# Feed-forward products by half products, with the convolution's sums in PSUM

## What is computed

```python
def conv_ffn(h, w_up, conv_w, conv_b, w_down, rows):
    u = h @ w_up                                   # (512, 1024) @ (1024, 5632)
    u = conv2d_grid(u, conv_w, rows) + conv_b      # 3x3, each channel by itself
    gate, val = jnp.split(u, 2, axis=-1)           # 2816 channels each
    return (jax.nn.silu(gate) * val) @ w_down      # (512, 2816) @ (2816, 1024)
...
        h = modulate(rms_norm(x, norm2_g[l]), sh2, sc2)
        x = x + g2 * conv_ffn(h, ffn_w_up[l], ffn_conv_w[l], ffn_conv_b[l], ffn_w_down[l], rows)
```

## Time and profile before

| | us |
|---|---|
| runs of the kernel before | 2051.56, 2053.72, 2055.73 |
| median | 2053.72 |
| the profiled execution's own time | 2056.36 |
| its span | 2054.4 |
| feed-forward, first to last up product | 582.95 to 889.10 |
| feed-forward, down products | 889.10 to 1065.20 |

### The profile page before, as it was taken

One profiled execution on the slowest core, in us unless ns is written; L12 is line 12 of the kernel. 1 busy time (PEld: TensorE's weight loads), 2 busy tenths in 40 slices (PEclk: granted clock), 3 DMA queues, 4 the chain that ended last, 5 costly groups with the idle time before them and its releaser, 6 DMA issues. The chain is left out here.

```text
span 2054.4 us, 27368 instructions
## 1 busy us (share of the span) xinstructions
PE 1844.3 (90%) x11650; PEld 1047.3 (51%) x11650; DVE 938.7 (46%) x1560; ACT 401.8 (20%) x740; POOL 152.0 (7%) x223
## 2 busy tenths in 40 slices
PE   6999759788999999999979999989988988878887
PEld 3554338676434444444538888865565333233332
DVE  2564196354349888950028559954443110101013
ACT  3222443234120111010113111253022000000001
POOL 0000002850000000000001100010000000000000
PEclk8999979798999999999989999999998999999999
DMA  8344004322311221135225522230538999999996
GB/s 318 139 184 153 21 21 108 82 53 78 106 60 67 82 82 68 63 102 193 87 82 200 210 103 82 98 109 21 208 149 319 427 426 426 426 426 425 427 427 251
DMA packets 80909, 375.40 MB, mean 183 GB/s; under 512 B 34336, under 2 KB 37408, under 8 KB 56848
## 3 DMA queue, kind: packets, MB, share of 16 engines
q1 hardware_dynamic: 68480, 344.56, 43.1%
q0 software_dynamic: 9552, 27.73, 3.8%
q10 hardware_dynamic: 2752, 1.31, 0.2%
HBM read 360.65 MB, written 18.87 MB: 185 GB/s over the span
## 5 line engine op out<-in xcount | busy, mean ns | idle before, releaser
L3113 PE MATMUL psum<-mem 128*64 128x512 f32 x1504 | 356.5, 630 | 36.3 <-DMA mem<-in_w_upe 16.3
L1962 PE MATMUL psum<-mem 128*128 128x512 f32 x704 | 305.0, 595 | 2.0 <-ACT mem L377 2.0
L1752 PE MATMUL psum<-mem 128*128 128x256 f32 x1120 | 250.4, 383 | 9.3 <-ACT mem L2330 4.9
L3113 PEld LDWEIGHTS psum<-mem 128*64 128x64 f32 x1504 | 117.9, 144 | 254.4 <-issue 250.9
L2028 DVE SCALAR_TENSOR_TENSOR mem<-mem 128x512 f32<-128x512 f32 x352 | 237.1, 750 | 0.0
L1752 PEld LDWEIGHTS psum<-mem 128*128 128x128 f32 x1120 | 212.7, 191 | 47.5 <-issue 13.9
L1962 PEld LDWEIGHTS psum<-mem 128*128 128x128 f32 x704 | 133.7, 190 | 172.7 <-issue 171.3
L574 PE MATMUL psum<-mem 128*128 128x512 f32 (+1 forms) x464 | 167.6, 523 | 2.1 <-ACT mem L377 2.0
L1408 PE MATMUL psum<-mem 128*128 128x512 f32 x352 | 156.0, 600 | 1.2 <-ACT mem L1984 1.2
L574 PEld LDWEIGHTS psum<-mem 128*128 128x128 f32 x464 | 87.9, 190 | 81.1 <-issue 72.1
L3175 DVE TENSOR_TENSOR mem<-mem,psum 128x512 f32<-128x512 f32 x16 | 11.0, 688 | 248.5 <-issue 217.9
(11 more groups left out here) (383 smaller groups left out, 2125.0 us busy)
## 6 DMA issues: line engine op xcount, KB each, us to landing
mem<-in_w_upe SPq DMA_DIRECT2D x31, 2048.0 KB, 27.5
mem<-in_w_gate SPq DMA_DIRECT2D x30, 2048.0 KB, 29.1
mem<-in_w_downe SPq DMA_DIRECT2D x29, 2048.0 KB, 32.2
mem<-in_ada SPq DMA_DIRECT2D x32, 1024.0 KB, 6.8
mem<-in_w_up SPq DMA_DIRECT2D x22, 1024.0 KB, 4.8
mem<-in_ada POOLq DMA_DIRECT2D x32, 512.0 KB, 4.8
mem<-in_w_in_g SPq DMA_DIRECT2D x12, 1024.0 KB, 4.9
mem<-in_w_down SPq DMA_DIRECT2D x16, 704.0 KB, 4.1
```

Source lines behind the costliest of these rows:

```text
L1752: last = pe.matmul(self.bank(q, n), left[:, kt], right[:, kt], start=n in (1, 2, 5) and kt == 0, stop=kt == self.tiles - 1, skip_group_che ...
L1962: last = pe.matmul(k.bank[2 * (m % 3) + h2][:, :], w[:, kt, h2], h[:, kt], start=kt == 0, stop=kt == KD - 1)
L3113: last = pe.matmul(bank[halves[h], :], xs[:, kt, halves[h]], pair[h][0][:, kt, cols], start=kt == 0, stop=kt == tiles - 1, skip_group_chec ...
```

## The change

The up products go by `Seven`, one pair for each m (gate tile and value tile, 4 input tiles in a quarter); the down products by `SevenDown`, four pairs of output tiles, 11 input tiles in a quarter. The weight quarters of the down products no longer pass through the ring: they have places of their own, which `SevenDown.load` fills (704 KB each). `x1` is updated in place.

The work around them moves:

- ACT reads out seven half results per pair (`take`): four into the padded grids, the three to be joined into `part`. It also starts each convolution: the centre tap with the bias, from the grid into a PSUM bank (`centre`).
- DVE does eight taps for each half, onto the sum in PSUM (banks 4 to 7); the last tap of the value half writes to SBUF. It makes t1 to t4 at the start.
- POOL makes the weight sums s1 to s4 of each pair, the three joins (`add`) and the product into `hidden`.
- The side jobs move to other places of the down half: all modulation rows stand between its first products.

```diff
+class SevenDown(SevenResidual):
...
+    def load(self, sp, q, i, j):
+        if (i, j) == (0, 0) and q:
+            sp.wait_ge(self.done[1], q)
+            sp.wait_ge(self.summed, 4 * q)
...
+        sp.dma_start(self.slot(q, i, j), self.source(q, i, j)).then_inc(self.landed[i, j], 16)
...
+    def sum_1(self, eng, q):
+        if q:
+            eng.wait_ge(self.done[7], q)
+            eng.wait_ge(self.summed, 4 * q)
...
+        eng.tensor_tensor(self.s1, self.block(q, 1, 0), self.block(q, 1, 1), ADD).then_inc(self.summed, 1)
...
+    def sum_3(self, eng, q):
+        eng.wait_ge(self.done[5], q + 1)
+        eng.tensor_tensor(self.s1, self.block(q, 0, 0), self.block(q, 1, 0), SUB).then_inc(self.summed, 1)
...
         @block.gpsimd
...
+            def add(q, n):
+
+                h2, j, other = {2: (0, 0, 1), 3: (0, 1, 6), 7: (1, 1, 5)}[n]
+                at = pads.half(h2, q, j)
+                pool.wait_ge(up.taken[other], q + 1)
+                pool.wait_ge(up.taken[n], q + 1)
+                pool.tensor_tensor(at, at, rows4(pads.part[n]), ADD).then_inc(s["added"], 1)
+
+            def product(m):
+                pool.wait_ge(s["silu"], m + 1)
+                pool.wait_ge(s["tap_v"], NT * (m + 1))
+                pool.tensor_tensor(hidden[:, m], pads.silu[m % 2], pads.value[m % 2], MUL).then_inc(s["hidden"], 1)
...
+            for q in range(KF):
+                if q:
+                    add(q - 1, 7)
+                if q >= 3:
+                    product(q - 3)
+                add(q, 2)
+                if q < LAST:
+                    landed(q + 1)
+                    up.sum_1(pool, q + 1)
+                    up.sum_2(pool, q + 1)
+                add(q, 3)
+                if q < LAST:
+                    up.sum_4(pool, q + 1)
+                    up.sum_3(pool, q + 1)
+                if q == LAST - 1:
+                    down.sum_1(pool, 0)
+            add(LAST, 7)
+            product(LAST - 2)
+            pool.wait_ge(up.done[4], KF)
+            pool.wait_ge(s["hidden"], 11)
+            down.turn_1(pool)
+            down.sum_2(pool, 0)
+            down.sum_4(pool, 0)
+            product(LAST - 1)
+            down.sum_3(pool, 0)
+            product(LAST)
 
         @block.tensor
...
+            for q in range(KF):
+                k.weights_ready(pe, k.number("w_up", q))
+                for n in (1, 2, 5, 6):
+                    up.product(pe, q, n, (lambda kt, first=4 * (n - 1): apply.ready(pe, first + kt, 0)) if q == 0 and n < 3 else None)
+                if q:
+                    up.product(pe, q - 1, 4)
+                up.product(pe, q, 3)
+                up.product(pe, q, 7)
+            up.product(pe, LAST, 4)
...
+            down.product(pe, 0, 1)
...
+            mod.rows_by_product(pe, range(4))
+            pe.wait_ge(up.taken[4], KF)
+            down.product(pe, 0, 5)
+            mod.rows_by_product(pe, range(4, 8))
+            pe.wait_ge(s["hidden"], KF)
+            down.product(pe, 0, 2)
+            mod.turn(pe)
...
         @block.scalar
...
+            def centre(h2, m):
+                act.wait_ge(s["added"], 3 * m + 2 + h2)
...
+                t = m + KF * h2
+                act.activation(pads.sums[h2](m), pads.inner(h2, m), ACT.Identity, bias=k.v("ffn_conv_b", t),
+                               scale=k.v("ffn_conv_w", CENTRE * 2 * KF + t)).then_inc(s[("centre_g", "centre_v")[h2]], 1)
...
+            for q in range(KF):
+                if q:
+                    centre(0, q - 1)
+                take(q, 1)
+                take(q, 2)
+                if q >= 2:
+                    silu(q - 2)
+                take(q, 5)
+                take(q, 6)
+                if q:
+                    take(q - 1, 4)
+                    centre(1, q - 1)
+                take(q, 3)
+                take(q, 7)
...
         @block.vector
...
+            def tap(h2, m, i):
+                done, centre = (s[("tap_g", "tap_v")[h2]], s[("centre_g", "centre_v")[h2]])
+                if i == 0:
+                    dve.wait_ge(centre, m + 1)
+                else:
+                    dve.wait_ge(done, NT * m + i)
...
+                dve.scalar_tensor_tensor(out=out, in0=pads.shifted(h2, m, TAPS[i]), scalar=w, in1=a, op0=MUL, op1=ADD).then_inc(done, 1)
...
+                if kt == 6:
+                    dve.wait_ge(apply.done, 4)
+                    up.turn_1(dve)
...
+            for m in range(KF + 1):
+                for i in range(NT):
+                    if m < KF:
+                        tap(0, m, i)
+                    if m:
+                        tap(1, m - 1, i)
```

More of the change, by code:

```diff
@@ L1942, in _, with landed @@
             sp.dma_start(context.x, k.d["ctx2"]).then_inc(context.landed, 16)
+            down.load(sp, 1, 0, 1)
             k.send_weights(sp)
+            for q in range(2, ND):
+                down.load(sp, q, 0, 1)
+                down.load(sp, q, 0, 0)
+                down.load(sp, q, 1, 0)
+                down.load(sp, q, 1, 1)
         @block.gpsimd
         def _(pool):
-            pool.memset(k.at(work, NP * 2 * PADW), 0.0).then_inc(s["zeroed"], 1)
-            pool.memset(mod.c32, 0.0).then_inc(s["zeroed"], 1)
+            def landed(q):
+                g = k.number("w_up", q)
+                pool.wait_ge(k.w_loaded[g % RING], 16 * (g // RING + 1))
@@ new lines, in _ @@
+            down.product(pe, 0, 3)
+            down.product(pe, 0, 7)
+            for q in range(1, ND):
+                down.product(pe, q, 1)
+                down.product(pe, q, 2)
+                if q == 2:
+                    context.sum(pe, 2)
+                down.product(pe, q, 5)
+                if q == 3:
+                    context.spread(pe)
+                down.product(pe, q, 6)
+                if q < 3:
+                    context.sum(pe, (0, 3)[q - 1])
+                down.product(pe, q - 1, 4)
+                down.product(pe, q, 3)
+                norm.sum(pe, 2 * q - 2)
+                down.product(pe, q, 7)
+                if q == 1:
+                    context.sum(pe, 1)
+                norm.sum(pe, 2 * q - 1)
@@ L1966, in _ @@
+            down.product(pe, ND - 1, 4)
+            norm.sum(pe, KD - 2)
             norm.sum(pe, KD - 1)
@@ new lines, in _, with square @@
+            centre(0, LAST)
+            take(LAST, 4)
+            centre(1, LAST)
+            silu(LAST - 1)
+            mod.take_rows(act, 0)
+            mod.take_rows(act, 1)
+            silu(LAST)
+            mod.take_rows(act, 2)
+            mod.take_rows(act, 3)
+            warm_root(k, act)
+            def square(m):
+                down.tile_done(act, m)
+                norm.square(act, m, x1[:, m])
+            act.wait_ge(mod.turned, 1)
+            square(0)
+            context.square(act, 0)
@@ L2000, in _ @@
+            context.square(act, 1)
+            square(1)
+            square(2)
+            context.square(act, 2)
+            context.square(act, 3)
+            context.take_root(act)
+            for m in range(3, KD):
+                square(m)
             act.wait_ge(s["total"], 1)
@@ new lines, in _ @@
+            add(0, 1)
+            dve.wait_ge(s["hidden"], KF)
+            down.turn_2(dve)
+            add(0, 5)
+            down.turn_3(dve)
+            add(0, 2)
+            add(0, 6)
+            down.turn_4(dve)
+            add(0, 3)
+            add(0, 7)
+            for q in range(1, ND):
+                down.sum_1(dve, q)
+                down.sum_2(dve, q)
+                down.sum_4(dve, q)
+                if q == 1:
+                    mod.add(dve)
+                add(q, 1)
+                add(q, 2)
+                add(q, 5)
+                down.sum_3(dve, q)
+                add(q, 6)
+                if q == ND - 1:
```

328 lines of the change are left out of this document (173 added, 155 removed).

## The result

| | before | changed |
|---|---|---|
| median of 4 runs each, one chip, us | 2054.56 (2051.56 to 2055.73) | 1997.72 (1991.55 to 2002.72) |
| ratio to before, 95% interval | | 0.9724 (0.9693 to 0.9755) |
| profiled execution, its span | 2056.36, 2054.4 | 1999.77, 1997.9 |
| feed-forward, from its first product to the start of the final norm's last product, its spread (L1970, now L2130) | 488.99 | 434.73 |
| of it up | 306.15 | 269.63 |

The change takes 56.8 us off the median. In the two profiled executions the feed-forward stage lost 54.3 us of the 56.6 between them. The rest is not the change's: the stage starts 2.7 us earlier (580.22 against 582.95), behind the same work, and what follows it is 0.5 us longer.

What follows compares the result with a forecast made beforehand. PE was taken to bound both feed-forward halves. Savings of 36.0 us up and 19.3 down sum to 55.3 off the 2053.7 us median, giving 1998.4, stated as 1999 us; range 1989 to 2025.

Steps and rivals of the forecast that it cites:

- A pair at 12.12 us: Up half: seven half products, 56 instructions at 0.2164 us, take 12.12 us of PE per pair.
- Up half: From first up product to the down half: 270.1 us instead of 306.15, so 36.0 us saved.
- The start: Start of the up half: 3.0 us lost, bounds 1.6 and 6, as product 2 waits for the eighth applied tile.
- The tap's period: Up half on DVE: sixteen taps a pair at 0.674 us, 10.8 us in all; high end 0.79 each, 12.6 us.
- rival (a): Up half: DVE becomes the bound at 0.79 us a tap, 11 us more, 2010 us in all; chance 0.12.
- GpSimd and ACT: Up half, per pair: GpSimd 8.2 us, about 8.9 with hand-overs, and ACT 5.1, both under 12.12.
- Rival (b): Up half: ACT or GpSimd holds PE 1 us each pair, 22 us more, 2021 us in all; chance 0.11.
- Contention: DVE taps beside GpSimd: no time charged, since taps have one operand in PSUM; only turns and weight sums at the start collide.
- Rival (c): Up half: taps and GpSimd exclude each other for whole instructions, 19.7 us a pair, 2165 us in all; chance 0.05.
- Down half: Down half: products 133.3 us instead of 151.4, saving 18.1; net saving with waits and tail 19.3 us.
- the wait for the rows' weights: Between the halves: PE waits 1.5 us, bounds 0 and 5, for the last weight tiles of the modulation rows.
- Rival (d): More gain: the 4.6 us at a lower clock and the start's 3 do not arise, 1992 us; chance 0.05.

Runs made afterwards that it cites:

- the eighth half product: Changed kernel with an eighth half product, its result unused, added to each up pair: 2027.19 us in one run.
- the two extra additions: Changed kernel with two more 512-word additions on GpSimd in each up pair: 1994.0 us; with four more, 2031.56 us.
- the rows moved alone: Changed kernel with the last two groups of modulation rows moved behind down product 2, GpSimd's order unchanged: 1999.64 us in one run.
- both moves: Changed kernel with half the modulation rows behind down product 2 and GpSimd's last product into `hidden` ahead of sum s3: median 1993.26 us, ratio 0.9723.

## Why the prediction was right

*The total.* 1997.7 us against 1999 forecast is closer than the sum behind it: the stage saved 54.3 us and not 55.3, the up half half a microsecond more and the down half 1.6 less, while the profiled executions differ by 56.6, of which 2.3 lie outside the stage. So the last microsecond or two of the match is luck; the mechanism is judged by the stage.

*A pair at 12.12 us.* Right to the digit, and the eighth half product shows that it is PE's time. Up half 269.6 us against 270.1 forecast: saved 36.5 against 36.0.

*The start.* 269.63 - 22 x 12.12 - 0.5 = 2.5 us lost, 3.0 forecast. It is the wait for the eighth tile, as forecast: ACT ends that tile at 585.39, where the forecast's time from the first product gives 585.5. PE's clock is 0.50 (1.2 GHz) until 584, as it was at the start of the stage before, but the tile comes later still. The turns did collide with GpSimd there, t1 too, which the prediction had left out (the sum beside it took 2.17 us). It cost PE nothing, though narrowly: t2 ends at 587.52, and the first weight load of product 6 is at 587.64.

*DVE.* The tap's period is 0.659, at the low end of the range; it decides rival (a) against. The reason given for it, that no tap needs the one right before it, is borne out too: the last pair's value taps have no gate taps between them, and seven of them take 864.82 - 859.29 = 5.53 us, 0.79 each, the figure of rival (a).

*GpSimd and ACT.* GpSimd's 512 words were mis-sized, 1.28 us against 1.17, and its 256 words 0.69 against 0.79; together 8.5 us a pair, within the 8.2 to 8.9 given. ACT's 7 x 0.384 + 2 x 0.78 + 0.59 = 4.8 against 5.1. Rival (b) is excluded by the waits and by the two extra additions. It is real at 13.6 us.

*Contention.* Nothing charged, and nothing found in steady state. Rival (c) was real for another placement of the sums, and priced 2.7 us a pair too dear (19.7 against 17.0), since it charged whole durations.

*Down half.* Saved 17.7 us against 19.3, and its terms were off in both directions. More time than forecast: the wait for the rows' weights 3.1 instead of 1.5; products at a lower clock 139.1 - 133.3 = 5.8 instead of the 4.6 kept from before (the row's 139.4 holds two instructions of the last up product); `mod.turn` in the same low stretch 4.8 instead of 3.9. Less: the last down product 4 did not wait (0.5; idle before L1723 is 0.1), the norm's sums and its spread are 1.0 shorter in busy time (5.1 and 1.6 us for 5.6 and 2.1), and the context's sums and spread 0.3. In sum -19.3 + 1.6 + 1.2 + 0.9 - 0.5 - 1.0 - 0.3 = -17.4, within 0.3 of what was measured. The wait of 1.2 before the first down product is gone as well, but it lay in the up half of before, 304.97 of 306.15 us busy, and is part of the 36.5.

The rows' weights are the term that missed most. The last of them was asked for where forecast, by 858.8, and landed at 869.5, some 11 us later and not 7.4. The t1 on GpSimd took 6.2 instead of 5.5 and ended at 856.4, before product 5 at 858.4. `hidden` was whole 20.8 us after product 7's end (847.6 to 868.5) against 19.5: the taps kept to the forecast, and the sum s3 in front of the last product on GpSimd is what it had left out. It cost PE nothing, since the rows' weights came later still. The down pairs came 34.7 and 36.7 us apart by DVE's first weight sums, instead of 33, since I gave the side jobs' time in the sum but not in that period. A weight sum of 1408 words takes 1.62 us, as the prediction has it, though the row it names would scale to 1.69.

*Rival (d)* did not come: the lower clock stayed, and even grew. With the rows moved alone PE waited as long as without, in one wait of 3.22 us for two of 1.71 and 1.41, and since the stages are equal too (434.1 and 434.7 us), it lost about as much to the clock. That the clock falls because of these waits is not shown: with both moves it is 1.00 until 874, some 13 us behind the only wait of over 0.5 us, and 0.73 in the 6 us after.

That the halves add up is shown by the kernel with the up half alone, to within 2 us. What stays open: why the clock falls at different instants in two runs of the same kernel (0.79 and 0.64 from 874 to 886 here; in the run again 0.51 from 862 to 868 and 0.72 from 874 to 880), and whether the both-moves version is truly 2 us better.

## What to carry to other kernels

A stage bound by one engine gives back what is taken from that engine, as long as the work of every other engine in a period stays below the new one. Here VectorE could be filled to 12.0 of 12.12 us and GpSimd to 11.0 without cost, and 13.6 us on GpSimd was too much. Where VectorE and GpSimd work side by side, put one of VectorE's two operands into PSUM: it was worth 112 us here, twice what the change gained. Where two halves join, look for the next thing that PE would wait for before moving work out of the first one's way, and allow for a low clock there.

## What was not expected of the hardware

- Two SBUF inputs beside GpSimd work stretched a tap from 0.74 to 1.1 to 1.8 us, and once to 6.03, GpSimd's 512 words from 1.28 to about 1.7, its 256 words from 0.69 to 1.14. The later one ends a fixed time after the earlier one's end: 0.55 us for the tap, 1.13 to 1.14 for 512 words on GpSimd. Only 0.14 to 0.19 us of a duration is hidden.
- A `tensor_scalar` from SBUF into PSUM has a period of 0.72 us (two in 1.44) and lasts 0.81, where the one before, SBUF to SBUF, has a period of 22.1/44 = 0.50 and lasts 0.55.
- ACT's centre tap, from SBUF into PSUM, takes 0.78 us for 512 words, and Silu from PSUM into SBUF 0.59. With the sums in SBUF, the same two take 0.81 and 0.63, so the difference is mostly the instruction's and not the place's.
- GpSimd's cost per word falls with length: 2.7 ns at 256 words (0.69 us), 2.5 at 512, 2.2 at 2816 (6.2 us).
